# Convolution blocks of a two-layer kernel: normalised with channels or with tokens on the partitions

## The chip, the core and the metric

One core of a Trainium2 chip runs the whole program. The metric is the device time of one execution in microseconds (us). Tensor names are those of the kernel; P is 128, the number of partitions; S is 512, the number of tokens.

## The reference

Two transformer layers over 512 tokens of width 1024. The change touches the first layer's convolution branch: GLU, a causal depthwise convolution of 31 taps over 512 channels, LayerNorm over each group of 128 channels, then SiLU.

```python
def conformer_conv(val_b, gate_b, conv_w, conv_b, ln_g, ln_b):
    g = val_b * jax.nn.sigmoid(gate_b)
    c = lax.conv_general_dilated(g, conv_w[:, None, :], window_strides=(1,), padding=[(CONV_W - 1, 0)],
        dimension_numbers=('NWC', 'WIO', 'NWC'), feature_group_count=D_B)
    c = c + conv_b
    c = layer_norm(c.reshape(bsz, seq, H_B, HD_B), ln_g.reshape(H_B, HD_B), ln_b.reshape(H_B, HD_B))
    return jax.nn.silu(c).reshape(bsz, seq, D_B)

mix = jnp.concatenate([a_out, b_out], axis=-1)       # a_out: spatial gating of u and v
x = x + jnp.einsum('bsc,cd->bsd', mix, w_out[l])
```

The first layer goes on with a feed-forward block (FF1, FF2); the second layer has attention and another feed-forward block.

## The kernel before

Activations lie with channels on the partitions and the 512 tokens along the free dimension. Each fp32 product is taken as three fp32r matmuls: weights and activations are split into a high and a low part (high x high, high x low, low x high). The weights come as a stream of 512 KB chunks into four slots. SyncE loads them (`raw`), GpSimd splits them into `wh` and `wl` (L412, L415), TensorE uses them in the same order. GpSimd may split chunk n only when chunk n - 4 has been used (`chunk_done`). Its order, with extra jobs between chunks, is the table `after_chunk` (L506): multiplying GLU gates, ten taps of block 3 (`conv_taps`), and `head_low(0)`, `(1)`, `(2)`, which write the low part of the normed blocks 0 to 2 (semaphore `mixb_low`) after chunks `C_U+2`, `C_OUT1+3` and `C_OUT1+6`.

TensorE's order in the first layer is: eight GLU chunks, four V chunks with tokens on the partitions (`group_natural`, L571), four U chunks with the token mixing `mix_tokens` after each (L691), the product with `w_out` in three parts, then FF1. The three parts are `out1_first` (rows of the gating branch, eight tiles of 12 matmuls), `out1_heads` (convolution blocks 0 to 2, eight tiles of nine matmuls) and `out1_last` (block 3, eight tiles of three matmuls, four of them ahead of FF1 and four between its first matmuls).

VectorE's order is written out by hand from L1693. A convolution tap is one instruction over 128x512: the first two of a block are products (L1591, L1593), every further one adds to one of two accumulators in PSUM by turns (L1596). `conv(n)` issues the next n taps; the other jobs (`v_moments`, `u_scale`, `shifted_mix`, `gated`, `out1_first` and so on, the evictions and the gating) stand between them. VectorE does 114 taps and GpSimd ten.

The norm of a block runs as follows. `conv_center` (L680) subtracts the mean over channels by a fp32 matmul with a centering matrix, once for each accumulator (and once for GpSimd's part of block 3). `head_in` (L1187) squares and copies it on ScalarE, `norm_sums` (L625) takes the mean of squares with four matmuls of one column, `norm_sd` the root, `norm_factor` (VectorE) the reciprocal, `norm_spread` (L674) spreads it over the partitions by four transposes, `head_scale` (L1609) multiplies, and `head_out` (L1196) applies gain, bias and SiLU on ScalarE and copies the high part. `out1_heads` waits for `mixb_low` k + 1 ahead of its part k, and takes tiles 0 to 3 in two passes: blocks 0 and 1 of all four, then block 2 of all four (L807 to L812).

On ScalarE the functions Sqrt, Gelu and SiLU each need their own table (ACT_TABLE_LOAD); Copy and Identity need no change of it.

## Time and profile before

| | us |
|---|---|
| median of three runs | 1173.28 |
| lowest and highest | 1173.26, 1176.16 |
| the profiled execution | 1173.25 |
| its span, first to last instruction | 1171.5 |

The profile's page gives each engine's busy time (first part) and the trace a timeline, a table by stretches, and lists of who waited for whom. PE is TensorE's matmuls, PEld its weight loads, DVE VectorE, ACT ScalarE, POOL GpSimd. A matmul's duration overlaps the next one's: in a steady stream 128x512 fp32r matmuls of 0.39 us start 0.23 us apart. A fp32 matmul that isn't fp32r has two records in the trace for one instruction of the kernel (x2).

| stage of the first layer (TensorE) | from us | to us |
|---|---|---|
| GLU | 5.6 | 55.3 |
| V | 55.3 | 80.2 |
| U and mixing | 80.2 | 106.2 |
| out1, gating rows | 107.9 | 134.6 |
| out1, blocks 0 to 2 | 137.2 | 154.9 |
| out1, block 3, first four tiles | 154.9 | 157.6 |

### The profile page before, as it was taken

To read this page: it belongs to the slowest core of one execution; us is meant where nothing else is said; L and a number is where in the kernel's file an instruction comes from. 1 tells how busy PE (TensorE), PEld (TensorE's weight loads), DVE (VectorE), ACT (ScalarE), POOL (GpSimd) and SP (SyncE) were. 2 spreads that over 40 slices of the span, in tenths; PEclk is the share of its full clock that TensorE was granted. 3 is DMA by queue.
4 is the path that set the end of the run, shared out by engine and by line. 5 is a ranking of instruction groups with operands and counts; after the bars stand their busy time and mean duration, and the time that the engine had idled before them with its cause. 6 is when DMAs were issued, how large, how long until landed. Compare 5 with 4: busy or idle time off the path is not lost.

```text
span 1171.5 us, 15607 instructions
## 1 busy us (share of the span) xinstructions
PE 1152.4 (98%) x5394; PEld 929.9 (79%) x5394; DVE 609.0 (52%) x1005; ACT 291.0 (25%) x575; POOL 712.5 (61%) x436
## 2 busy tenths in 40 slices
PE   7999999999999999999999998999999999999997
PEld 5888788888888888888777776777888888888886
DVE  4999665530024443458789778847454001454114
ACT  5144352210001211120212346546421000221111
POOL 7879848666666666656455433226976666665660
PEclk9999999999999999999999999999999999999999
DMA  7321223322323223224433221112232322323312
GB/s 253 115 91 55 90 71 127 107 90 92 106 90 103 94 91 107 90 90 135 121 113 102 78 83 55 34 46 73 89 108 90 106 92 90 107 90 98 100 36 72
DMA packets 35760, 110.73 MB, mean 95 GB/s; under 512 B 4992, under 2 KB 7168, under 8 KB 35712
## 3 DMA queue, kind: packets, MB, share of 16 engines
q1 hardware_dynamic: 32352, 105.40, 27.0%
q10 hardware_dynamic: 3360, 4.69, 1.6%
q8 instruction: 30, 0.49, 0.2%
q14 instruction: 18, 0.15, 0.0%
HBM read 102.47 MB, written 2.10 MB: 89 GB/s over the span
## 4 chain that ended last, share of the span: by engine, by line
PE 92%; DVE 6%; issue 1%; ACT 1%; DMA 0%; DVEq 0%; SPq 0%; ACTq 0%
PE bank L554 25%; PE bank L556 25%; PE bank L555 25%; DVE bank L1596 2%; PE bank L926 2%; PE bank L586 1%; PE bank L585 1%; PE bank L587 1%; PE bank L619 1%; PE bank L611 1%; PE bank L612 1%; PE bank L940 1%; PE bank L968 1%; PE bank L884 1%; PE bank L964 1%
## 5 line engine op out<-in xcount | busy, mean ns | idle before, releaser
L415 POOL TENSOR_TENSOR wl<-raw,wh 128x1024 fp32r<-128x1024 f32 x188 | 454.8, 2419 | 15.7
L412 POOL TENSOR_SCALAR wh<-raw 128x1024 fp32r<-128x1024 f32 x188 | 202.8, 1079 | 394.8 <-PE bank L556 276.2
L554 PE MATMUL bank<-xh,wh 128*128 128x512 f32 x776 | 307.9, 397 | 0.4 <-ACT va L1332 0.4
L556 PE MATMUL bank<-xh,wl 128*128 128x512 f32 x776 | 302.5, 390 | 0.0
L555 PE MATMUL bank<-xl,wh 128*128 128x512 f32 x776 | 302.3, 390 | 0.0
L554 PE MATMUL bank<-uh,wh 128*128 128x512 f32 (+1 forms) x560 | 215.3, 384 | 0.0
L556 PE MATMUL bank<-uh,wl 128*128 128x512 f32 (+1 forms) x560 | 214.5, 383 | 0.0
L555 PE MATMUL bank<-ul,wh 128*128 128x512 f32 (+1 forms) x560 | 214.5, 383 | 0.0
L554 PEld LDWEIGHTS bank<-xh,wh 128*128 128x128 f32 x776 | 145.7, 188 | 45.7 <-issue 16.5
L1810 DVE TENSOR_TENSOR ul<-tmb,uh 128x512 f32 x64 | 124.7, 1948 | 90.1 <-ACT uh L1277 90.1
L556 PEld LDWEIGHTS bank<-xh,wl 128*128 128x128 f32 x776 | 145.7, 188 | 31.1
L555 PEld LDWEIGHTS bank<-xl,wh 128*128 128x128 f32 x776 | 145.8, 188 | 28.8 <-issue 0.2
L1276 ACT ACTIVATE tmb<-tmp 128x512 f32<-128x512 f32 x64 | 40.4, 632 | 413.3 <-DVE tmp L1807 413.3
L555 PEld LDWEIGHTS bank<-ul,wh 128*128 128x128 f32 x560 | 105.3, 188 | 20.8 <-issue 0.2
L556 PEld LDWEIGHTS bank<-uh,wl 128*128 128x128 f32 x560 | 105.2, 188 | 20.8
L554 PEld LDWEIGHTS bank<-uh,wh 128*128 128x128 f32 x560 | 105.3, 188 | 20.6 <-issue 0.2
L1807 DVE SCALAR_TENSOR_TENSOR tmp<-bank,rb 128x512 f32<-128x512 f32 x64 | 44.1, 688 | 70.7 <-PE bank L556 66.1
L1596 DVE SCALAR_TENSOR_TENSOR bank<-gpad,cols,bank 128x512 f32<-128x512 f32 x98 | 66.7, 749 | 0.0
L1821 DVE TENSOR_TENSOR x<-bank,x 128x512 f32 x8 | 5.5, 692 | 78.1 <-PE bank L556 78.1
L1823 DVE COPY y<-bank 128x512 f32 x8 | 5.5, 692 | 78.1 <-PE bank L556 78.1
L1277 ACT ACTIVATE uh<-tmp 128x512 f32 x64 | 39.5, 617 | 0.0
L585 PE MATMUL bank<-wh,xh 128*128 128x512 f32 x96 | 38.0, 395 | 0.0
(278 smaller groups left out, 1218.4 us busy)
## 6 DMA issues: line engine op xcount, KB each, us to landing
raw<-wstream SPq DMA_DIRECT2D x188, 512.0 KB, 3.3
x<-xT SPq DMA_DIRECT2D x8, 256.0 KB, 4.8
out<-x SPq DMA_DIRECT2D x16, 128.0 KB, 1.7
qi<-ropey ACTq DMA_DIRECT2D x16, 64.0 KB, 2.1
qd<-ropey ACTq DMA_DIRECT2D x16, 64.0 KB, 2.1
kd<-ropey ACTq DMA_DIRECT2D x16, 64.0 KB, 2.0
qa<-ropey SPq DMA_DIRECT2D x16, 64.0 KB, 2.0
ka<-ropey SPq DMA_DIRECT2D x16, 64.0 KB, 2.0
```

Of the source, the lines that this page charges most:

```text
L412: nc.gpsimd.tensor_scalar(wh[c][:], raw[c][:], 1.0, 1.0, ALU.mult, ALU.mult).then_inc(high_ready, 1)
L415: nc.gpsimd.tensor_tensor(wl[c][:], raw[c][:], wh[c][:].bitcast(F32), ALU.subtract).then_inc(split_ready, 1)
L554: mm(out, wh_, mh, start=start, stop=False)
L555: mm(out, wh_, ml, start=False, stop=False)
L556: return mm(out, wl_, mh, start=False, stop=stop)
L585: mm(out, xh[:, k, ts], wh[s][:, ws], start=k == 0, stop=False)
L926: mm(bank[4 + e][:, 0:N], q[r, h, tb * P:tb * P + P], k[r, h, 0:N], start=True, stop=True).then_inc(scores_done, 1)
L1276: A(tmb[c][:], tmp[c][:], ACT.Square).then_inc(square_ready, 1)
L1277: A(uh[:, bass.ds(r * 4 + c, 1), :].rearrange("p a n -> p (a n)"), tmp[c][:], ACT.Square).then_inc(uh_ready, 1)
L1596: ins = V.scalar_tensor_tensor(out=out, in0=src, scalar=w, in1=acc, op0=ALU.mult, op1=ALU.add)
L1807: V.scalar_tensor_tensor(out=tmp[c][:], in0=bank[c][:], scalar=0.0, in1=rb[:], op0=ALU.max, op1=ALU.mult).then_inc(evacuated, 1)
L1810: V.tensor_tensor(ul[:, bass.ds(r * 4 + c, 1), :].rearrange("p a n -> p (a n)"), tmb[c][:], uh[:, bass.ds(r * 4 + c, 1), :].rearrange("p a ...
```

## The change

The mean and the variance of a convolution block are taken with tokens on the partitions. VectorE adds the two accumulators (`conv_sum`), TensorE turns the block by four 128x128 transposes into `bank[4]` (`head_turn`), VectorE takes statistics over the 128 channels of each token (`head_moment`: four `bn_stats`, four `bn_aggr`), ScalarE the root (`head_root`), VectorE reciprocal and shift (`head_factors`), ScalarE norms in four instructions with scale and bias (`head_norm`), TensorE turns back into `NB` (`head_return`), and `head_out` reads that. Centering matrix, squares, one-column sums, spreads and `head_scale` go. The first two taps of blocks 1 to 3 are done by ScalarE (`head_first_taps`). The orders on TensorE, ScalarE and VectorE are written anew; blocks 0 to 2 of `out1_heads` are no longer taken in two passes. GpSimd's order stays; it builds two constants fewer. Semaphore counts shared with later norms are kept up by larger increments (`HEAD_NORMS`, left out below).

```diff
         vg = at("vg", [P, TB, 512], F32, uh_at + half + 8192)
-        conv_a = at("conv_a", [P, 2, S], F32, ul_at + half)
-        conv_o = at("conv_o", [P, 2, S], F32, ul_at + half + 4096)
+        conv_s = at("conv_s", [P, 2, S], F32, ul_at + half)
...
+            def head_turn(h):
+                pe.wait_ge(conv_summed, h + 1)
                 if h:
-                    pe.wait_ge(cm_ready, h)
-                pe.wait_ge(conv_step, (h + 1) * TAPS - (POOL_TAPS if h == 3 else 0))
-                mm(bank[4][:], center[:], conv_a[:, h % 2], start=True, stop=False)
-                if h == 3:
-                    pe.wait_ge(conv_pool, POOL_TAPS)
-                    mm(bank[4][:], center[:], conv_p[:], start=False, stop=False)
-                mm(bank[4][:], center[:], conv_o[:, h % 2], start=False, stop=True).then_inc(centered, 1)
+                    pe.wait_ge(head_normed, TB * h)
+                for t in range(TB):
+                    ts = slice(t * P, t * P + P)
+                    last = nc.tensor.transpose(bank[4][:, ts], conv_s[:, h % 2, ts], ident[:])
+                last.then_inc(head_turned, 1)
+            def head_return(h):
+                pe.wait_ge(head_normed, TB * (h + 1))
+                if h == 0:
+                    pe.wait_ge(mix_shifts, 4)
+                else:
+                    pe.wait_ge(silu_ready, h)
+                for t in range(TB):
+                    ts = slice(t * P, t * P + P)
+                    last = nc.tensor.transpose(NB[:, ts], cm[:, h % 2, ts], ident[:])
+                last.then_inc(head_returned, 1)
...
-            group_natural(C_V, 0, E_V - 4, between=(lambda: conv_center(0), first_head_sums, lambda: norm_spread(1)))
...
-                chunk_transposed(n % SLOTS, bank[m][:], xh, xl)
+                chunk_transposed(n % SLOTS, bank[m][:], xh, xl, hooks={4: lambda: head_turn(1)} if m == 0 else {})
                 if m:
                     mix_tokens(m - 1)
             mix_tokens(3)
-            conv_center(1)
+            head_return(1)
...
-                    if 3 * o + k in (5, 15, 23):
+                    if 3 * o + k in (7, 15, 23):
...
             for o in range(8):
                 out1_first(o)
-                if o == 0:
-                    norm_sums(2, sq[1], 1, head_sq, 2)
-                if o == 1:
-                    norm_spread(2)
-                if o == 3:
-                    conv_center(2)
                 if o == 4:
-                    norm_sums(3, sq[0], 1, head_sq, 3)
-                if o == 5:
-                    norm_spread(3)
-            conv_center(3)
+                    head_turn(2)
+                if o == 6:
+                    head_return(2)
             for o in range(4):
-                out1_heads(o, range(2))
-            norm_sums(4, sq[1], 1, head_sq, 4)
-            for o in range(4):
-                out1_heads(o, range(2, 3))
-            norm_spread(4)
-            for o in range(4, 8):
+                out1_heads(o, range(3))
+            head_turn(3)
+            for o in range(4, 6):
+                out1_heads(o, range(3))
+            head_return(3)
+            for o in range(6, 8):
                 out1_heads(o, range(3))
             for o in range(4):
                 out1_last(o)
...
-            def head_in(h):
-                act.wait_ge(centered, h + 1)
+            def head_first_taps(j):
+                act.wait_ge(conv_summed, j)
+                act.wait_ge(glu_ready, j + 1)
+                t = POOL_TAPS if j == 3 else 0
+                A(conv_acc[0][:], gpad[:, j, t:t + S], ACT.Identity, scale=col("conv_w", j * TAPS + t),
+                  bias=col("conv_b", j)).then_inc(first_taps, 1)
+                t += 1
+                A(conv_acc[1][:], gpad[:, j, t:t + S], ACT.Copy, scale=col("conv_w", j * TAPS + t)
+                  ).then_inc(first_taps, 1)
+            def head_root(h):
+                act.wait_ge(head_moments, TB * (h + 1))
+                A(head_mv[:, :, 2:3], head_mv[:, :, 1:2], ACT.Sqrt, bias=eps[:, 0:1]).then_inc(head_std, 1)
+            def head_norm(h):
+                act.wait_ge(head_factor, h + 1)
                 if h >= 2:
-                    act.wait_ge(bc_used, h)
-                    act.wait_ge(sums_done, h)
-                A(sq[h % 2][:], bank[4][:], ACT.Square).then_inc(head_sq, 1)
-                A(cm[:, h % 2], bank[4][:], ACT.Copy).then_inc(cm_ready, 1)
+                    act.wait_ge(head_returned, h - 1)
+                for t in range(TB):
+                    ts = slice(t * P, t * P + P)
+                    A(cm[:, h % 2, ts], bank[4][:, ts], ACT.Identity, scale=head_mv[:, t, 3:4],
+                      bias=head_mv[:, t, 4:5]).then_inc(head_normed, 1)
             def head_out(h):
-                act.wait_ge(bc_used, h + 2)
+                act.wait_ge(head_returned, h + 1)
                 if h >= 2:
                     act.wait_ge(mixb_low, h - 1)
                 else:
                     act.wait_ge(glu_ready, h + 3)
                 out = bank[4] if h == 3 else tmb[2 + h % 2]
-                A(out[:], tmp[2 + h % 2][:], ACT.Silu, scale=col("conv_g", h), bias=col("conv_lb", h)
+                A(out[:], NB[:], ACT.Silu, scale=col("conv_g", h), bias=col("conv_lb", h)
                   ).then_inc(silu_ready, 1)
...
             for j in range(4):
                 sigmoid(j)
-            head_in(0)
-            norm_sd(1)
+            head_first_taps(1)
+            head_root(0)
+            head_norm(0)
             head_out(0)
             for t in range(TB):
                 v_gelu(t)
+            head_first_taps(2)
             act.wait_ge(v_stats, TB)
             A(mvs[:, :, 2:3], mvs[:, :, 1:2], ACT.Sqrt, bias=eps[:, 0:1]).then_inc(v_std, 1)
+            head_root(1)
             act.wait_ge(v_factor, 1)
             for t in range(TB):
                 A(vg[:, t], vg[:, t], ACT.Identity, scale=mvs[:, t, 3:4], bias=mvs[:, t, 4:5]).then_inc(v_normed, 1)
+            head_norm(1)
             for h in range(4):
                 u_gelu(h)
                 if h:
                     a_high(h - 1)
             a_high(3)
-            head_in(1)
-            norm_sd(2)
             head_out(1)
             A(soft[:, 0:1], eps[:, 0:1], ACT.Sqrt).then_inc(table_loaded, 1)
-            head_in(2)
-            norm_sd(3)
+            head_first_taps(3)
+            head_root(2)
+            head_norm(2)
             head_out(2)
             A(soft[:, 0:1], eps[:, 0:1], ACT.Sqrt).then_inc(table_loaded, 1)
-            head_in(3)
-            norm_sd(4)
+            head_root(3)
+            head_norm(3)
             head_out(3)
...
             steps = [0]
-            DVE_TAPS = [(j, t) for j in range(4) for t in range(POOL_TAPS if j == 3 else 0, TAPS)]
...
-                        dve.wait_ge(centered, j - 1)
-                    acc = conv_acc[i % 2][:]
+                    acc = conv_acc[first % 2][:]
                     src = gpad[:, j, t:t + S]
                     w = col("conv_w", j * TAPS + t)
-                    if i >= 2:
+                    if j and first < 4:
+                        dve.wait_ge(first_taps, 2 * (j - 1) + first - 1)
+                    elif i >= 2:
                         dve.wait_ge(conv_step, i - 1)
                     if first == 0:
                         ins = V.tensor_scalar(acc, src, w, col("conv_b", j), ALU.mult, ALU.add)
                     elif first == 1:
                         ins = V.tensor_scalar(acc, src, w, None, ALU.mult)
                     else:
-                        out = (conv_o if t % 2 else conv_a)[:, j % 2] if t >= TAPS - 2 else acc
+                        if t == TAPS - 2 and j >= 2:
+                            dve.wait_ge(head_turned, j - 1)
+                        out = conv_s[:, j % 2] if t == TAPS - 2 else acc
                         ins = V.scalar_tensor_tensor(out=out, in0=src, scalar=w, in1=acc, op0=ALU.mult, op1=ALU.add)
                     ins.then_inc(conv_step, 1)
                 steps[0] += taps
+            def conv_sum(j):
+                assert steps[0] == len([1 for jj, _ in DVE_TAPS if jj <= j])
+                dve.wait_ge(conv_step, steps[0])
+                total = conv_s[:, j % 2]
+                if j < 3:
+                    V.tensor_tensor(total, conv_acc[0][:], total, ALU.add).then_inc(conv_summed, 1)
+                else:
+                    link(V.tensor_tensor(conv_acc[0][:], conv_acc[0][:], total, ALU.add))
+                    dve.wait_ge(conv_pool, POOL_TAPS)
+                    V.tensor_tensor(total, conv_acc[0][:], conv_p[:], ALU.add).then_inc(conv_summed, 1)
+            def head_moment(h):
+                dve.wait_ge(head_turned, h + 1)
+                for t in range(TB):
+                    V.bn_stats(head_stats[:, t, 0:6], bank[4][:, t * P:t * P + P]).then_inc(head_counted, 1)
+                for t in range(TB):
+                    dve.wait_ge(head_counted, TB * h + t + 1)
+                    V.bn_aggr(head_mv[:, t, 0:2], head_stats[:, t, 0:6]).then_inc(head_moments, 1)
+            def head_factors(h):
+                dve.wait_ge(head_std, h + 1)
+                dve.wait_ge(head_moments, TB * (h + 1))
+                link(V.reciprocal(head_mv[:, :, 3:4], head_mv[:, :, 2:3]))
+                V.scalar_tensor_tensor(out=head_mv[:, :, 4:5], in0=head_mv[:, :, 0:1], scalar=-1.0,
+                                       in1=head_mv[:, :, 3:4], op0=ALU.mult, op1=ALU.mult).then_inc(head_factor, 1)
             def u_scale(j):
                 dve.wait_ge(chunk_done, C_U + j + 1)
...
                     dve.wait_ge(sig_ready, 4)
                 mul(tmp[j % 2][:], bank[j % 4][:], rb[:]).then_inc(evacuated, 1)
-            def head_scale(h):
-                dve.wait_ge(bc_done, h + 2)
-                if h >= 2:
-                    dve.wait_ge(silu_ready, h - 1)
-                mul(tmp[2 + h % 2][:], cm[:, h % 2], NB[:]).then_inc(bc_used, 1)
             def head_low(h):
                 dve.wait_ge(mixb_high, h + 1)
...
             gate(3)
             conv(1)
+            conv_sum(0)
             shift_of_mix()
-            conv(18)
-            norm_factor(1)
-            conv(8)
-            head_scale(0)
-            conv(8)
+            conv(10)
+            head_moment(0)
+            conv(4)
+            head_factors(0)
+            conv(15)
+            conv_sum(1)
             for t in range(TB):
                 v_moments(t)
-            conv(3)
+            head_moment(1)
+            u_scale(0)
+            conv(2)
             v_factors()
-            u_scale(0)
-            conv(7)
+            head_factors(1)
+            conv(4)
             u_scale(1)
             conv(1)
             shifted_mix(0)
...
             gated_low(0)
             conv(4)
             u_scale(2)
-            conv(1)
             shifted_mix(1)
             gated(1)
             conv(1)
             gated_low(1)
-            conv(3)
+            conv(4)
             u_scale(3)
             shifted_mix(2)
             gated(2)
...
             gated(3)
             conv(1)
             gated_low(3)
-            conv(4)
+            conv(2)
             out1_first(0)
-            conv(2)
-            norm_factor(2)
-            conv(2)
+            conv(3)
             out1_first(1)
-            head_scale(1)
             conv(3)
             out1_first(2)
             conv(3)
+            conv_sum(2)
             out1_first(3)
-            conv(6)
+            conv(3)
             out1_first(4)
+            conv(3)
+            head_moment(2)
+            out1_first(5)
             conv(2)
-            norm_factor(3)
+            head_factors(2)
             conv(2)
-            out1_first(5)
-            head_scale(2)
+            out1_first(6)
             conv(3)
-            out1_first(6)
             out1_first(7)
-            assert steps[0] == 4 * TAPS - POOL_TAPS
-            norm_factor(4)
-            for k in range(4):
+            conv(3)
+            out1_heads(0)
+            conv(3)
+            conv_sum(3)
+            for k in range(1, 4):
                 out1_heads(k)
-            head_scale(3)
+            head_moment(3)
             out1_heads(4)
+            head_factors(3)
             out1_heads(5)
             head_low(3)
```

## Rows read from the trace of the kernel before

**Rows 1.** Page, first part: busy time, share of the span, instructions of each engine
```profile
PE 1152.4 (98%) x5394; PEld 929.9 (79%) x5394; DVE 609.0 (52%) x1005; ACT 291.0 (25%) x575; POOL 712.5 (61%) x436
```

**Rows 2.** Table by stretch: us, then busy us of each engine, granted clock, DMA share, GB/s
```profile
55.00:80.00 25.00, 25.00 (x114) 20.08 (x114) 24.86 (x42) 8.77 (x12) 16.36 (x10) 1.00 0.26 89
80.00:105.00 25.00, 24.84 (x122) 20.84 (x120) 24.70 (x44) 9.95 (x14) 23.68 (x16) 1.00 0.22 79
105.00:137.00 32.00, 31.78 (x143) 24.10 (x143) 28.82 (x47) 14.14 (x20) 30.97 (x21) 1.00 0.18 59
```

**Rows 3.** Who waited for whom, TensorE, whole run: us in total, times, longest
```profile
PE bank L611 <- ACT xh L1168: 5.6, 1, 5.6
PE bank L940 <- DVE probs L2023: 1.9, 3, 1.2
...
PE bank L697 <- DVE tmp L1502: 0.3, 1, 0.3
```

**Rows 4.** Who waited for whom, GpSimd, 80.54 to 139.45 us: the only entry
```profile
POOL wh L412 <- PE bank L587: 1.1, 1, 1.1
```

**Rows 5.** Timeline, GpSimd: start us, us, engine line op out<-in, idle before
```profile
80.54 1.05 POOL L412 TENSOR_SCALAR wh<-raw 128x1024 fp32r<-128x1024 f32 x1 [1.10 <-PE bank L587]
...
138.15 1.30 POOL L475 TENSOR_TENSOR ul<-tmb,uh 128x512 fp32r<-128x512 f32 x1
```

**Rows 6.** Timeline, TensorE: centering, sums, spread, and the start of FF1
```profile
60.71 1.02 PE L685 MATMUL bank<-conv_a,center 128*128 128x512 f32 x2
...
62.66 0.40 PE L586 MATMUL bank<-wl,xh 128*128 128x512 f32 x1
...
67.92 0.95 PE L631 MATMUL bank<-inv,sq 128*128 128x1 f32 x8
...
69.05 0.39 PE L586 MATMUL bank<-wl,xh 128*128 128x512 f32 x1
...
74.30 0.60 PE L671 MATMUL bank<-ident,rn 128*128 128x128 f32 x4
...
74.97 0.39 PE L586 MATMUL bank<-wl,xh 128*128 128x512 f32 x1
...
157.62 0.39 PE L611 MATMUL bank<-xh,wh 128*128 128x512 f32 x1
```

**Rows 7.** One line of the kernel: attention's turns, ns min/median/max, first and last start
```profile
L940 PE MATMUL bank<-ident,probs x120: 270/272/330, 649.5 to 777.1; 128*128 128x128 f32 x120
```

**Rows 8.** Timeline, VectorE
```profile
56.73 1.12 DVE L1640 SCALAR_TENSOR_TENSOR mix_shift<-bank,cols,rows 128x128 f32<-128x128 f32 x4
...
69.76 5.33 DVE L1596 SCALAR_TENSOR_TENSOR bank<-gpad,cols,bank 128x512 f32<-128x512 f32 x8
...
78.89 0.81 DVE L1591 TENSOR_SCALAR bank<-gpad,cols 128x512 f32<-128x512 f32 x1
...
80.92 0.69 DVE L1625 BATCH_NORM_STATS2 stats<-vg 128x6 f32<-128x512 f32 x1
81.64 0.18 DVE L1626 BATCH_NORM_AGGREGATE mvs<-stats 128x2 f32<-128x6 f32 x1
...
93.85 0.70 DVE L1502 TENSOR_TENSOR bank<-bank,ug 128x512 f32<-128x512 f32 x1
...
104.45 0.68 DVE L1502 TENSOR_TENSOR tmp<-bank,rb 128x512 f32<-128x512 f32 x1
```

**Rows 9.** Timeline, ScalarE
```profile
86.70 2.94 ACT L1237 ACTIVATE vg<-vg,mvs 128x512 f32<-128x512 f32 x4 [2.15 <-DVE mvs L1632]
89.65 1.28 ACT L1211 ACT_TABLE_LOAD   x1
```

**Rows 10.** Timeline, TensorE, shortly after its first matmul
```profile
9.25 0.63 PE L612 MATMUL bank<-xh,wl 128*128 128x512 f32 x1
...
10.04 0.39 PE L611 MATMUL bank<-xh,wh 128*128 128x512 f32 x1
10.27 0.40 PE L612 MATMUL bank<-xh,wl 128*128 128x512 f32 x1
```

More of the change, by code:

```diff
@@ L43 @@
 POOL_TAPS = 10
+HEAD_NORMS = 4
 HEADS = 8
@@ L636, in norm_sums @@
                                   start=True, stop=True)
-                last.then_inc(sums_done, 1)
+                last.then_inc(sums_done, 1 + HEAD_NORMS if i == 0 else 1)
             def head_sums(h):
@@ L1150, in norm_rb @@
                 act.wait_ge(bc_done, i + 1)
-                A(out[:], NB[:], ACT.Copy).then_inc(bc_used, 1)
+                A(out[:], NB[:], ACT.Copy).then_inc(bc_used, 1 + HEAD_NORMS if i == 0 else 1)
             squares = [0]
@@ L1573, in _ @@
             steps = [0]
-            DVE_TAPS = [(j, t) for j in range(4) for t in range(POOL_TAPS if j == 3 else 0, TAPS)]
+            DVE_TAPS = [(j, t) for j in range(4) for t in range((POOL_TAPS if j == 3 else 0) + (2 if j else 0), TAPS)]
             def conv(taps):
```

45 lines of the change are left out of this document (20 added, 25 removed).

## The prediction

> **What bounds the kernel now.** The page's first part comes first: TensorE is busy for 98% of the span, so a change pays only where it takes work or waiting off TensorE [rows 1]. The table by stage then shows the part that the change touches, 55 to 157 us. From 55 to 137 us two engines are nearly full at once: TensorE without gaps, and VectorE for 24.86 of 25, 24.70 of 25 and 28.82 of 32 us; GpSimd joins them from 80 us (23.68 of 25, 30.97 of 32) [rows 2]. The list of waits has only one entry of TensorE between 24 and 157 us, the 0.3 us ahead of the last mixing matmuls [rows 3]. GpSimd waited once between 80.54 and 139.45 us, at its start, for the last V matmul, and then ran without a wait up to the low part of convolution block 2 [rows 4, 5]. That start and that end carry the forecast. Everything after about 158 us (FF1 onward) the change leaves alone, and TensorE bounds it, so I let a shift at the start of FF1 pass 1:1 to the end.
>
> **TensorE: what goes and what comes.** A centering is two fp32 128x512 matmuls: the first starts at 60.71 us, and the first V matmul in regular step behind it at 62.66 (0.23 a matmul) instead of 60.94, so 1.72 us; block 3 has a third, 2.58. Four make 7.7 us. The four sums with one column: 67.92 to 69.05 less 0.23 is 0.90 us, four 3.6. The four spreads: 74.30 to 74.97 less 0.23 is 0.44, one with a small wait, 2.0 in all [rows 6]. Removed: 13.4 us. Added are eight groups of four 128x128 transposes. The nearest rows are the spreads (same form, 0.44 a group) and the 120 turns of attention's probabilities, which carry data as these do, 272 ns long and pipelined [rows 6, 7]. I take 0.44, together 3.5 us; the ends are 0.44 and four times 0.272, 1.09. The net is 9.9 us: 1173.25 - 9.9 = 1163.4 if TensorE alone decided.
>
> The rows show 272 ns as a duration that overlaps its neighbours. The Trainium skill (TensorE: Matmul & The Clock Gate, Part 4: PE-mode transpose) puts a 128x128 bf16 transpose at about 275 ns inside a kernel; the duration agrees, but if this were also the distance from one to the next, the groups would cost 8.8 us, an estimate, and the net 4.6.
>
> **VectorE.** Gone: six first taps, about 0.69 each (0.72 and 0.66), 4.1 us; four scalings of 512 elements, 0.60 each in step (0.70 long, as the products are), 2.4; four reciprocals, 0.4. Added: five sums of the two accumulators at 0.60 to 0.69, 3.1; sixteen statistics over 128 elements, sixteen aggregations at 0.10 in step, and four pairs of factors, 0.35 each. The statistics' price isn't in the trace: 512 elements take 0.66, another 128-element instruction takes 0.26 in step. Bounds 0.10 and 0.66; I take 0.22, as the length scales [rows 8]. A block's moments are then 4 x 0.22 + 4 x 0.10 + 0.1 for the first wait = 1.4 us. Added: 3.1 + 5.6 + 1.4 = 10.1, net 3.2 us more on an engine that had no slack from 57 to 134 us. Six taps move behind `out1_first(6)`, where it did have slack.
>
> **ScalarE.** Four normalising instructions replace Square and Copy. Four of 512 elements with scale and bias take 2.94 us; less 384 elements at 0.83 ns each leaves 0.4, so 1.6 us a block. A tap 0.75. The table for Gelu or Silu loads only behind them, 1.28 [rows 9].
>
> **Along the stages.** (1) Up to V. V0 ends at 60.71. `conv_sum(0)` is done at 57.5, so the turn costs 0.44. VectorE: mix shifts to 58.5, ten taps at 0.655 to 65.1, moments 66.5, four taps 69.1, factors 69.5; ScalarE's norm is ready at 71.2. TensorE reaches `head_return(0)` at 61.15 + 2 x 5.44 = 72.03, no wait, 0.8 us of margin. V3 ends at 77.9 where it ended at 80.2: 2.3 us early (1.72 - 0.44 and 0.90, remainder rounding; spread against return is even).
>
> (2) GpSimd. Its unbroken run starts with V3's end, 2.3 us early, and none of its conditions (chunks 13 to 18 done, `mixb_high`) comes later than its own pace. `head_low(2)`, 138.15 to 139.45 now, then ends at 137.2 [rows 5]. No edit touches this order.
>
> (3) Gelu and mixing. VectorE after the factors of block 0: fifteen taps and `conv_sum(1)` to 80.0, V moments 83.2, head moments 84.6, `u_scale(0)` 85.2, two taps, `v_factors` 87.15, factors 87.5. ScalarE's V norm ends at 90.1 and `head_norm(1)` at 91.7 now stands ahead of the Gelu table: first Gelu done at 93.6 (before, the table loaded at 89.65 and the first Gelu was done at 91.6), so `gated(0)` starts at 93.65 against 93.85 and VectorE waits 1.5 us. `mix_tokens(0)` waits until 90.1, 0.85 us on TensorE. `u_scale(3)` ends at 104.9 against 105.05, so the last mixing starts only about 0.2 us early [rows 8, 9]. TensorE's lead has gone into waits for VectorE and ScalarE.
>
> (4) First half of out1. Its first tile ends at 110.1, as against 110.67. Without the sums and the spread, `out1_first(6)` ends at 126.9. VectorE: two taps, then a tile and three taps in turn, `conv_sum(2)` 119.4, moments 126.3, factors 128.6; ScalarE's norm 130.2. `head_return(2)` stands in TensorE's queue ahead of `out1_first(7)`, so TensorE waits about 3.4 us. Return 130.7, `out1_first(7)` 133.4, two parts of `out1_heads(0)` 134.8.
>
> (5) The gate. The third part needs `mixb_low` 3, because blocks 0 to 2 are no longer taken in two passes. Silu and copy are ready at 133, but GpSimd delivers at 137.2. TensorE waits 2.4 us. From there: 0.68, three tiles of 2.04 to 144.0, turn 144.4, two tiles 148.5; VectorE: tile 3, moments 146.1, tile 4, factors 147.65; norm 149.3, so `head_return(3)` waits 0.8; 149.8, two tiles: 153.9. Before, this point lay at 154.9 (four `out1_last` tiles of 0.68 ahead of FF1's 157.62) [rows 6]. Block 3's Silu, copy and low part end at 152.7, ahead of their reader.
>
> Shift: 1.0 us. Span 1170.5, time 1173.25 - 1.0 = 1172.2. The profiled execution is 1.75 us longer than its span and equals the median (1173.28) for this purpose.
>
> **Rivals.**
>
> A, *the last norm is hidden*: as above, but `head_return(3)` finds it ready. 149.0 + 4.08 = 153.1, 1.8 us early: 1171.4. This is also the floor that the GpSimd gate allows.
>
> B, *small instructions cost more than their length*: statistics at the upper bound, 0.66. Each block's moments grow by 1.6 us. `head_return(0)` then waits 0.8, V3's end and the gate go to 138.0; up to block 2 VectorE is 4.8 us later, more than the 2.4 us of slack at the gate, so TensorE passes it at 139.7; block 3 adds another 1.6. Sum: -1.0 + 2.5 + 1.6 = +3.1, time 1176.3, slower. For it: nothing shows 128-element statistics. Against: other 128-element rows scale down [rows 8]. It turns the sign once moments cost about 0.9 us more than I take. Transposes 0.27 apart would add 0.65 at each of two groups ahead of V's end and of two behind the gate: 1174.8.
>
> C, *TensorE's clock falls in the new waits*. At the start, after 5.6 us of idling, matmuls take 0.63 us and come about 0.4 us apart until 10 us, then 0.39 long and 0.23 apart, which fits 1.2 and then 2.4 GHz (the granted-clock column itself reads 1.00 over this stretch, so I go by the matmuls). The nine slow ones cost about 1.8 us [rows 3, 10]. The new waits are 3.4 and 2.4 us, the longest since then. A slow stretch after the first is absorbed by the gate; one after the second costs 1.8: 1174.0, slower than now. Within the kernel's body no wait was longer than 1.2 us [rows 3], so nothing here shows what 3 us do.
>
> The Trainium skill (TensorE: Matmul & The Clock Gate, Part 1) says that an idle spell throttles the array back to half rate until it has been busy again, which speaks against a change that trades matmuls for waits; no row here shows it inside the kernel.
>
> D, *TensorE alone decides*: 9.9 us less, 1163.4. It would need `mixb_low` 3 at 127 us, while GpSimd is full to 137.
>
> **How the numbers follow.** Forecast 1172.2: 45%. A 15%. B 15%, of which I give half a result beyond 1176.8. C 18%. D and anything else below 1169.8: 7%. The predicted time is 1172.2. The range takes in A's floor with 0.6 below it and reaches B's price: 1170.6 to 1176.3. About 0.3%, 3.5 us, is what a measurement tells from no change. Faster by more: 7%. Slower by more (above 1176.8): half of B and a case of B with C, 11%. Within: 82%.
>
> **What would show it.** TensorE's waits in 80 to 150 us: one under 1 us before the first mixing, one of about 3 us before the transposes of `head_return(2)`, one of 2 to 3 us before a matmul of `out1_heads(0)`, released by GpSimd's low part at 137.2, one under 1 us before `head_return(3)`. Transposes in step of 0.11. Statistics in step of 0.22. V3's last matmul about 2.3 us earlier. FF1's first matmul at 156.6. Wrong would be: GpSimd's run broken by a wait, statistics above 0.4, or matmuls 0.4 us apart after the waits.

## The result, and the profile after the change

| us | before | changed |
|---|---|---|
| median, 19 executions of each | 1173.37 | 1175.56 |
| lowest and highest | 1173.14, 1176.16 | 1175.35, 1176.56 |
| the profiled execution, its span | 1173.25, 1171.5 | 1176.56, 1174.8 |
| FF1's first matmul starts | 157.62 | 160.91 |

The ratio is 1.0018, 95% interval 1.0012 to 1.0024: 2.2 us slower, where 1.1 us faster was forecast. The profiled span grew by 3.3 us, and FF1 starts 3.3 us later, so all of it arises before FF1, as [rows 6] let it be read. The profiled execution of the changed kernel is its longest, 1.0 us above its median, so times read from this trace overstate the median's loss by about that much.

TensorE's work did fall. First the page's first part, then the list of waits of TensorE from 20 to 162 us, its only entries (us in total, times, longest):

```profile
PE 1147.6 (98%) x5360; PEld 927.1 (79%) x5360; DVE 614.5 (52%) x1036; ACT 295.5 (25%) x588; POOL 711.5 (61%) x434
```

```profile
PE bank L700 <- ACT cm L1210: 3.7, 2, 3.1
PE bank L709 <- ACT vg L1257: 3.4, 1, 3.4
PE bank L761 <- ACT uh L1241: 1.2, 1, 1.2
```

Busy time fell by 4.8 us against [rows 1], and that although some matmuls ran slower (below); [rows 3] had one wait of 0.3 in this stretch, now there are 8.3 us. L709 is the mixing, which waits for ScalarE's norm of V, L700 the return of a block, L761 the first half of out1. The table by stretch (granted clock third from the right) names the second loss:

```profile
90.00:105.00 15.00, 11.91 (x49) 10.15 (x50) 12.49 (x21) 8.25 (x14) 14.38 (x11) 0.77 0.21 70
105.00:120.00 15.00, 13.77 (x70) 11.23 (x70) 14.74 (x23) 6.34 (x9) 14.57 (x11) 1.00 0.13 47
120.00:135.00 15.00, 12.15 (x56) 9.72 (x54) 14.68 (x31) 3.00 (x7) 14.48 (x10) 1.00 0.25 81
135.00:140.00 5.00, 4.75 (x16) 3.85 (x17) 2.56 (x4) 4.38 (x6) 2.37 (x2) 0.66 0.42 147
```

Behind each of the two long waits the clock falls. The timeline of TensorE:

```profile
93.09 2.08 PE L709 MATMUL bank<-sguw,vg 128*128 128x128 f32 x8 [3.37 <-ACT vg L1257]
...
95.39 0.63 PE L556 MATMUL bank<-xl,wh 128*128 128x512 f32 x1
95.82 0.63 PE L557 MATMUL bank<-xh,wl 128*128 128x512 f32 x1
...
135.25 0.66 PE L700 MATMUL bank<-ident,cm 128*128 128x128 f32 x4 [3.11 <-ACT cm L1210]
...
136.75 0.63 PE L762 MATMUL bank<-uh,wl 128*128 128x512 f32 x1
137.18 0.63 PE L761 MATMUL bank<-uh,wh 128*128 128x512 f32 x1
```

Matmuls 0.63 long and 0.43 apart (1.2 GHz) in place of 0.39 and 0.23 (2.4 GHz), until 98.4 and again until about 139.3.

What made V's norm late stands on VectorE. Its timeline, then GpSimd's, of the same microseconds:

```profile
87.32 0.18 DVE L1674 RECIPROCAL mvs<-mvs 128x4 f32<-128x4 f32 x1
87.53 0.17 DVE L1522 TENSOR_TENSOR mvs<-mvs 128x4 f32<-128x4 f32 x1
87.74 2.34 DVE L1676 TENSOR_SCALAR mvs<-mvs 128x4 f32<-128x4 f32 x1
89.99 0.17 DVE L1647 RECIPROCAL head_mv<-head_mv 128x4 f32<-128x4 f32 x1
90.19 0.54 DVE L1648 SCALAR_TENSOR_TENSOR head_mv<-head_mv 128x4 f32<-128x4 f32 x1
```

```profile
87.66 2.39 POOL L416 TENSOR_TENSOR wl<-raw,wh 128x1024 fp32r<-128x1024 f32 x1
90.03 1.56 POOL L490 TENSOR_SCALAR ss<-gpad,cols 128x512 f32<-128x512 f32 x1
```

Each of these instructions handles four numbers per partition, and the last of the three instructions takes 2.34 us. It started 0.08 us behind a GpSimd split and ended (90.08) with it (90.05). V's norm therefore ends at 93.0, not 90.1.

### The profile page after: what moved, and what is told of

Same layout as the page of the kernel before. It is cut to its first block, busy times and chain, and to the rows that moved or that the text cites. A ratio compares the mean times of both kernels' runs of the same rounds, so it can differ in the third digit from the quotient of the medians.

```text
span 1174.8 us, 15580 instructions
## 1 busy us (share of the span) xinstructions
PE 1147.6 (98%) x5360; PEld 927.1 (79%) x5360; DVE 614.5 (52%) x1036; ACT 295.5 (25%) x588; POOL 711.5 (61%) x434
## 4 chain that ended last, share of the span: by engine, by line
PE 90%; DVE 7%; ACT 1%; issue 1%; DMA 0%; DVEq 0%; SPq 0%; ACTq 0%
PE bank L555 26%; PE bank L556 25%; PE bank L557 25%; DVE bank L1618 3%; PE bank L926 2%; PE bank L587 1%; PE bank L586 1%; PE bank L588 1%; PE bank L620 1%; PE bank L612 1%; PE bank L613 1%; PE bank L940 1%; PE bank L968 1%; PE bank L884 1%; PE bank L964 1%
## 5 line engine op out<-in xcount | busy, mean ns | idle before, releaser
L1618 DVE SCALAR_TENSOR_TENSOR bank<-gpad,cols,bank 128x512 f32<-128x512 f32 x102 | 69.9, 748 | 0.3 <-ACT bank L1192 0.3
L1875 DVE TENSOR_TENSOR y<-bank,y 128x512 f32<-128x512 f32 x7 | 4.8, 692 | 62.7 <-PE bank L557 62.7
```

The lines of the kernel that those rows point to most:

```text
L1618: ins = V.scalar_tensor_tensor(out=out, in0=src, scalar=w, in1=acc, op0=ALU.mult, op1=ALU.add)
```

## The experiments

Two theories stood at the start. The port (for the access to SBUF that the two engines would share): a small VectorE instruction with both operands, or source and target, in SBUF stands still while a GpSimd split runs, and its price isn't 0.17 but what is left of GpSimd's. The clock: the waits would be harmless, and what costs is the half rate behind them. Two rivals: the turns, statistics and norms themselves cost more than taken; or the order of the work around the return of block 2 is to blame.

**port_free.** The second operand of each pair of factors comes from PSUM, which holds a second copy of the reciprocal. V's factors are formed in the same way: two reciprocals and one product with -1 in place of reciprocal, product and negation. VectorE also waits (`silu_ready`) until `NB` is free to hold the copy.

```diff
-link(V.reciprocal(head_mv[:, :, 3:4], head_mv[:, :, 2:3]))
+if h:
+    dve.wait_ge(silu_ready, h)
+V.reciprocal(head_mv[:, :, 3:4], head_mv[:, :, 2:3])
+link(V.reciprocal(NB[:, 0:4].unsqueeze(2), head_mv[:, :, 2:3]))
 V.scalar_tensor_tensor(out=head_mv[:, :, 4:5], in0=head_mv[:, :, 0:1], scalar=-1.0,
-                       in1=head_mv[:, :, 3:4], op0=ALU.mult, op1=ALU.mult).then_inc(head_factor, 1)
+                       in1=NB[:, 0:4].unsqueeze(2), op0=ALU.mult, op1=ALU.mult).then_inc(head_factor, 1)
...
```

> The changed kernel, with the factors of the V norm and of the convolution norms formed so that no VectorE instruction on 128x4 has two SBUF inputs or goes from SBUF to SBUF with a constant: the reciprocal is also written to PSUM and the product reads it there. Theory 1 (the small instructions wait for a GpSimd instruction in flight: 2.34 us for a negation of 128x4, ended 0.03 us behind GpSimd's): each takes 0.2 us, the V norm starts near 87.4 instead of 90.1 us, the wait before the first mixing falls from 3.4 to about 0.9 us, the granted clock stays full from 90 to 105 us, and the time is 1172.3 to 1173.3 us (the second wait of about 3 us stays). Theory 2 (the small instructions are slow for a reason of their own, or VectorE has no time for them anyway): durations of 0.5 to 2.3 us stay or the lead is lost elsewhere, 1175.5.

Measured: 1172.77 us (1172.56 to 1174.37), ratio to before 0.9994, interval 0.9985 to 1.0004; span 1170.8, where the forecast had 1170.5. Its waits of TensorE from 20 to 162 us:

```profile
PE bank L700 <- ACT cm L1210: 3.1, 2, 2.5
PE bank L555 <- POOL ul L476: 1.7, 1, 1.7
PE bank L761 <- ACT uh L1241: 1.0, 1, 1.0
PE bank L709 <- DVE tmp L1522: 0.8, 1, 0.8
PE bank L612 <- issue: 0.2, 1, 0.2
```

The wait of 3.4 for V's norm is gone, and the gate of the forecast is there. GpSimd's timeline and TensorE's at that point:

```profile
135.99 1.26 POOL L476 TENSOR_TENSOR ul<-tmb,uh 128x512 fp32r<-128x512 f32 x1
```

```profile
137.40 0.47 PE L555 MATMUL bank<-uh,wh 128*128 128x512 f32 x1 [1.73 <-POOL ul L476]
```

The clock still fell behind the wait of 2.5 (0.89 in the stretch from 120 to 135 us), but the gate swallowed it. FF1 starts at 157.01. So 3.9 of the 4.3 us between the forecast's 156.6 and the changed kernel's 160.91 go with four VectorE instructions of 128x4; by the medians it is 2.8 us (1175.56 to 1172.77). V's factors need care here. They ran from 86.20 to 86.64, before the split began at 87.61, because block 0's pair no longer lost 1.35 us. Whether freeing block 0's pair alone would do the same wasn't tried. Nor is port_free faster than before, clear of noise: its interval includes no change.

**port_v.** The same for V's factors alone.

> The changed kernel with the second operand of V's factors alone taken from PSUM (the head blocks' pairs of factors stay as the change has them). If the loss comes from the one instruction that stood 2.34 us behind GpSimd's split, V's factors are done near 86.5, the mixing doesn't wait for ScalarE's norm, and the time is that of the kernel with both kinds of factors from PSUM but for the part of block 2, whose pair was stretched by 0.7: head_return(2) waits 3.1 to 3.3 (2.5 there) and the gate of 137.4 swallows that again, so 1172.8 to 1173.3. If the head blocks' pairs are a cause of their own, half of the 2.8 us or more stays: 1174.2 or above.

Measured: 1173.13 us (1172.73 to 1174.48), ratio 0.9997, 0.9987 to 1.0006; the wait of L700 3.3. The first range, 1172.8 to 1173.3, holds in time but not in every step: V's factors were done at 87.85, not 86.5, since block 0's pair still took its 1.51, and the mixing waited 1.1 us for V's norm, where no wait was expected. Its timeline shows the theory better than its time does. VectorE, with block 0 and then V and block 1:

```profile
69.23 1.51 DVE L1648 SCALAR_TENSOR_TENSOR head_mv<-head_mv 128x4 f32<-128x4 f32 x1
...
87.69 0.16 DVE L1677 SCALAR_TENSOR_TENSOR mvs<-mvs,bank 128x4 f32<-128x4 f32 x1
87.77 0.18 DVE L1647 RECIPROCAL head_mv<-head_mv 128x4 f32<-128x4 f32 x1
87.98 2.18 DVE L1648 SCALAR_TENSOR_TENSOR head_mv<-head_mv 128x4 f32<-128x4 f32 x1
```

and GpSimd:

```profile
68.33 2.39 POOL L416 TENSOR_TENSOR wl<-raw,wh 128x1024 fp32r<-128x1024 f32 x1
...
87.74 2.40 POOL L416 TENSOR_TENSOR wl<-raw,wh 128x1024 fp32r<-128x1024 f32 x1
```

The head factors, left in SBUF, took over the stretch of 2.18 and again ended with the split (90.16 and 90.14). In port_free the same instruction with a PSUM operand ran at the same moment, inside the same split, in 0.16 (VectorE, then GpSimd):

```profile
69.22 0.16 DVE L1651 SCALAR_TENSOR_TENSOR head_mv<-head_mv,bank 128x4 f32<-128x4 f32 x1
```

```profile
68.25 2.41 POOL L416 TENSOR_TENSOR wl<-raw,wh 128x1024 fp32r<-128x1024 f32 x1
```

1.51 against 0.16 is the cleanest pair: same data, same start, same neighbour. V's own factors, at 87.69, are no such proof, since they started just before the split. The other traces repeat both halves. Block 2's product with both operands in SBUF took 0.86 (changed kernel), 1.03 (port_v), 1.66 (warm) and 0.60 us (two_pass), and each time its end lay within 0.03 us of the end of a GpSimd instruction. In the changed kernel that was the first half of a split, which makes `wh` (VectorE, then GpSimd):

```profile
132.80 0.86 DVE L1648 SCALAR_TENSOR_TENSOR head_mv<-head_mv 128x4 f32<-128x4 f32 x1
```

```profile
132.60 1.04 POOL L413 TENSOR_SCALAR wh<-raw 128x1024 fp32r<-128x1024 f32 x1
```

With the operand in PSUM it took 0.16 inside a split in nine_same too (127.55). The theory is too wide at one point: the reciprocal goes from SBUF to SBUF, and in the changed kernel it took 0.17 at 68.93, inside a split that began at 68.23.

**warm.** The changed kernel, with three fp32 matmuls on constants in front of the first mixing and three in front of `head_return(2)`, so that TensorE works instead of waiting.

```diff
+                if m == 1:
+                    pe.wait_ge(evacuated, E_U + 1)
+                    keep_warm(3)
                 if m:
                     mix_tokens(m - 1)
...
                 if o == 6:
+                    pe.wait_ge(evacuated, E_OUT1 + 4)
+                    keep_warm(3, 3)
                     head_return(2)
```

> The changed kernel, with three fp32 matmuls of no use (0.86 us each) put ahead of the first mixing and three ahead of the turning back of block 2, where TensorE waited 3.4 and 3.1 us. Theory 1 (half of the loss is the clock): the granted clock stays at its full level in 90 to 105 and 135 to 140 us, the 12 and 9 matmuls that were 0.43 us apart come 0.23 apart, and the time is 1172.5 to 1173.2. Theory 2 (what counts is only when VectorE and ScalarE deliver): the time stays at 1175.5, the waits only move behind.

Measured: 1174.01 us (1173.90 to 1174.64), ratio 1.0001, 0.9991 to 1.0011. VectorE's instruction is as slow as before (2.34 at 88.02), the same norm is awaited, but no clock falls. The table by stretch and the mixing in TensorE's timeline:

```profile
90.00:105.00 15.00, 14.24 (x66) 10.78 (x65) 13.73 (x23) 8.58 (x14) 14.38 (x11) 1.00 0.21 70
...
135.00:140.00 5.00, 5.00 (x24) 4.10 (x24) 3.84 (x7) 3.59 (x5) 4.01 (x4) 1.00 0.43 153
```

```profile
93.38 1.16 PE L709 MATMUL bank<-sguw,vg 128*128 128x128 f32 x8 [0.76 <-ACT vg L1262]
```

FF1 starts at 158.50, 2.4 us before that of the changed kernel, and the profiled span is 2.5 shorter (1172.3). The median gained 1.6. So the two falls of the clock cost 1.6 us together by the medians and up to 2.4 in the profiled execution, and matmuls that compute nothing gave it back. I had expected 1172.5 to 1173.2, so the clock was worth less than I thought.

**port_warm.** Both edits.

> Both edits: the factors by way of PSUM, and the matmuls of no use ahead of the first mixing and of the turning back of block 2. If the port and the clock together are the whole difference from the forecast, the time is 1172.2 (1171.8 to 1172.6), the forecast for the change. If a third cause is at work, it stays at 1173 or above. The three matmuls ahead of the first mixing may be longer than the wait that is left there and cost up to 1.5 us of TensorE, which the wait at block 2 should absorb.

Measured: 1172.86 us (1172.62 to 1174.12), ratio 0.9992, 0.9983 to 1.0002, FF1 at 157.02, the gate's wait 1.7 again. That lies between my two cases (1171.8 to 1172.6, or 1173 and above). Against port_free nothing is gained: the one fall left there (behind the wait of 2.5) lies in front of the gate. Here the gate sets the time and the clock doesn't.

**two_pass.** The changed kernel, with `head_return(2)` behind `out1_first(7)`, the first four tiles of the heads in two passes (blocks 0 and 1, then block 2), `head_turn(3)` between them, and `head_return(3)` behind the fifth tile. VectorE's order follows.

```diff
...
-                if o == 6:
+                if o == 7:
                     head_return(2)
             for o in range(4):
-                out1_heads(o, range(3))
+                out1_heads(o, range(2))
             head_turn(3)
-            for o in range(4, 6):
-                out1_heads(o, range(3))
+            for o in range(4):
+                out1_heads(o, range(2, 3))
+            out1_heads(4, range(3))
             head_return(3)
...
```

> The changed kernel with TensorE's order in out1 altered: block 2 is turned back behind out1_first(7) instead of ahead of it, tiles 0 to 3 of the convolution rows are taken in two passes again (blocks 0 and 1, then block 2), block 3 is turned between the passes and turned back behind tile 4; VectorE's order follows. The waits at the factors and the first clock loss stay. If the order around block 2 is where the change loses its 10 us of TensorE work, the second wait shrinks from 3.1 to under 1 us, the second clock loss goes, and the time is 1170.2 (1169.5 to 1171.5). If VectorE is the bound whatever the order, it is 1174 to 1175.5.

Measured: 1173.97 us (1172.84 to 1175.46), ratio 0.9998, 0.9989 to 1.0008. The wait for block 2 is gone, and a wait of 2.2 for block 3's sum has taken its place; behind it the clock falls too (TensorE's timeline):

```profile
143.56 1.12 PE L688 MATMUL bank<-ident,conv_s 128*128 128x128 f32 x4 [2.24 <-DVE conv_s L1633]
144.33 0.78 PE L555 MATMUL bank<-uh,wh 128*128 128x512 f32 x1
144.91 0.63 PE L556 MATMUL bank<-ul,wh 128*128 128x512 f32 x1
```

So the order was worth something (1.6 by the medians), but far from the 1170.2 that I had expected: my first order of it turned block 3 too early. The four small instructions were left as slow as they were.

**nine_taps, nine_same.** With port_free's factors: one tap of block 3 moved from GpSimd to VectorE, to test the gate. nine_taps leaves out more than the expectation for nine_same says. With nine taps on GpSimd the two accumulators change places, and the sum still reads the first one: it counts ten taps twice and leaves out eleven. nine_same reads the other one and has all 31. Both issue the same instructions over the same sizes.

```diff
-POOL_TAPS = 10
+POOL_TAPS = 9
...
             out1_heads(0)
-            conv(3)
+            conv(4)
             conv_sum(3)
```

and in nine_same also

```diff
-                    link(V.tensor_tensor(conv_acc[0][:], conv_acc[0][:], total, ALU.add))
+                    link(V.tensor_tensor(conv_acc[0][:], conv_acc[1][:], total, ALU.add))
```

> With both kinds of factors from PSUM, and one tap of block 3 moved from GpSimd to VectorE. It tests the gate of the forecast: that GpSimd's unbroken run ends with head_low(2) at 137.2 and that TensorE's first use of that part waits for it. GpSimd has about 2.1 us less to do (a product of 1.57 and a sum), VectorE 0.66 more. If the gate holds as a price, TensorE's wait for GpSimd's low part (1.7 us at 137.40) goes to 0, what remains late is the return of block 2 (a wait of 2.5 in front of it), and the time falls by 1.0 to 1.7: 1171.1 to 1171.8. If the gate hides a wait that appears elsewhere (the turn or return of block 3, or VectorE's added tap), it stays within 0.4 of 1172.8.

> The kernel with both kinds of factors from PSUM and nine taps of block 3 on GpSimd, its sums now taken so that all 31 taps are in. The run with nine taps showed FF1's first matmul at 155.8 (157.0 with ten taps) but a median 2.9 us lower, 1.7 more than that step. If the 1.7 belong to the moved tap, the time is 1169.7 again. If they came from the part of the block that was missing there (the last tap of block 3 was outside the sum), or from an execution to execution difference behind FF1, FF1 starts at 155.8 again and the time is 1171.3 to 1171.8. The same for the gate itself in both cases: TensorE has no wait for GpSimd's low part of block 2.

Measured: nine_taps 1169.85 us (1169.66 to 1173.15), ratio 0.9967, 0.9955 to 0.9980; nine_same 1170.67 (1169.50 to 1172.77), ratio 0.9975, 0.9965 to 0.9984. In nine_same GpSimd starts the low part at 132.92 where port_free had 135.99, TensorE has no wait for it any more, and FF1 starts at 155.03, 2.0 earlier; the median is 2.1 lower. The gate was real, and its price slightly above the wait that showed it. Both expectations missed in time: nine_taps came out below its 1171.1, and nine_same between its two cases (1169.7, or 1171.3 to 1171.8). I had argued from nine_taps' profiled execution, and that was an odd one, 1173.15 where the other five took 1169.7 to 1170.8. In it VectorE lost 2.1 us early on (last section), and FF1 started at 155.80, 0.8 later than in nine_same. Behind FF1 it lost another 1.8 us, in the second layer's attention, where the granted clock was 0.50 from 725 to 730 us (nine_same 1.00). Why nine_taps' median is 0.8 below nine_same's stays open. The sum that it leaves out saves no instruction, and both kernels have executions at 1169.5 to 1169.8.

**two_late, two_again.** port_free's factors, the two passes, but `head_turn(3)` behind the second pass and `head_return(3)` behind the sixth tile. It ran twice. TensorE's order against that of two_pass:

```diff
             for o in range(4):
                 out1_heads(o, range(2))
-            head_turn(3)
             for o in range(4):
                 out1_heads(o, range(2, 3))
+            head_turn(3)
             out1_heads(4, range(3))
+            out1_heads(5, range(3))
             head_return(3)
```

> With both kinds of factors from PSUM, block 2 returned behind the last first-half tile, the heads' products of the first four tiles in two passes (parts 0 and 1, then part 2), block 3 turned after the second pass and returned before the seventh tile. It removes both what TensorE waits for ahead of the heads: 2.5 us before the return of block 2 and 1.7 at GpSimd's gate. If these waits are on the path and nothing stands behind them, FF1 starts 4.2 us earlier than at 157 and the time is 1168.6 to 1169.5. If the chain of block 3 is next (its sum is done near 143.5, and turn, statistics, root, norm, return, SiLU, copy and low part take some 7.5 us before its product can start), or GpSimd's splits of the next weights, only 1 to 2.5 us are gained: 1170.3 to 1171.8.

> The kernel with two passes and block 3 turned late once more, on the chip of the kernels with nine taps: FF1's first matmul at 152.1, 5.5 us before that of the kernel before, so 1167.8 to 1169.6 and a ratio of 0.995 to 0.996. A ratio above 0.9975 would say that the first result was one of its few runs.

Measured: 1168.63 (1167.73 to 1169.61), ratio 0.9958, 0.9941 to 0.9974, and 1168.69 (1167.94 to 1169.34), ratio 0.9957, 0.9940 to 0.9973. No chain of block 3 stood behind. One kernel, and its eight executions lie at 1167.7 to 1168.1 or 1169.3 to 1169.6. The two profiled ones, one of each kind, show what differs in them (TensorE's timeline at the gate, two_late, then two_again):

```profile
137.48 0.47 PE L555 MATMUL bank<-uh,wh 128*128 128x512 f32 x1 [1.06 <-POOL ul L476]
137.79 0.40 PE L556 MATMUL bank<-ul,wh 128*128 128x512 f32 x1
```

```profile
137.46 0.63 PE L555 MATMUL bank<-uh,wh 128*128 128x512 f32 x1 [2.00 <-POOL ul L476]
137.88 0.63 PE L556 MATMUL bank<-ul,wh 128*128 128x512 f32 x1
```

The gate opens at the same moment. TensorE reached it 0.9 us earlier in the second, waited 2.0 instead of 1.1, lost its clock, and started FF1 at 153.70 instead of 152.13. Arriving early cost 1.6 us. That the other six divide in the same way is likely, but no trace shows it.

**two_norm.** two_late, and ScalarE norms block 1 behind its last copy of the gated half, to reach the first GELU sooner. TensorE turns block 1 back behind the second tile of the gating rows (left out below).

```diff
-            head_norm(1)
             for h in range(4):
                 u_gelu(h)
                 if h:
                     a_high(h - 1)
             a_high(3)
+            head_norm(1)
             head_out(1)
...
```

> As the kernel with two passes and block 3 turned late, and in addition ScalarE norms block 1 behind its last copy of the gated half, and TensorE returns it behind the second first-half tile. ScalarE reaches the first GELU 1.5 us earlier (VectorE waited 1.3 for it before gated(0)). If the gated half is on the path into the first output tiles, TensorE's wait for its low part (1.0 us) goes and the time is 0.6 to 1.3 below that kernel. If VectorE's own order (the scalings of U and the taps) sets the first output tile, it is within 0.4 of it, and if block 1's later low part reaches the heads, above it.

Measured: 1169.36 (1167.76 to 1169.70), ratio 0.9962, 0.9948 to 0.9976. The lowest execution and both profiled spans (1166.0) are those of two_late, the medians of so few executions 0.7 apart. By the profiled executions that is the second case; by the medians the third isn't excluded. TensorE's waits in the gating rows are 1.5 us there (1.0 in two_late), so ScalarE's place in front of the first GELU gained nothing.

**two_nine.** two_late with nine taps on GpSimd, summed as in nine_same.

> The kernel with two passes and block 3 turned late (FF1 at 152.1, TensorE waits 1.1 us for GpSimd's low part of block 2, between the first and the second pass), with nine taps on GpSimd. If that wait is the last that stands in front of the heads, FF1 starts at 151.0 and the time is 1.1 us below the kernel with ten taps. If VectorE's tap, 0.66 more before the sum of block 3, moves the turn of block 3 and through it the last product, the gain is 0.4 or less.

Measured: 1166.02 us, all four executions between 1165.94 and 1166.15, ratio 0.9936, 0.9919 to 0.9953. It beats both kernels, by 7.6 us against the 1173.62 of before in these runs. TensorE's waits from 20 to 162 us:

```profile
PE bank L761 <- ACT uh L1243: 1.0, 1, 1.0
PE bank L709 <- DVE tmp L1524: 0.8, 1, 0.8
PE bank L612 <- issue: 0.2, 1, 0.2
```

FF1 starts at 150.43, 7.2 us before that of the kernel before. I expected 151.0 and a gain of 1.1 us; the median gained 2.7 over two_again. Part of it is the upper of two_again's two levels, which is missing here: TensorE doesn't wait at the gate any more, and in the profiled execution its clock stays full from 20 to 150 us. Against the lower level of the kernel with ten taps the gain is 1.7 to 2.1 us.

## Why the prediction was wrong, point by point

**The step that failed: "four pairs of factors, 0.35 each", and V's three at their old price.** Block 0's pair took 0.17 and 1.52, V's last 2.34, block 1's second 0.54, block 2's 0.86; only block 3's stayed at 0.17, and it had started 0.03 us ahead of GpSimd's next instruction (151.82 and 151.85). The first delay led to the longest one. Block 0's 1.35 us too many let V's factors begin at 87.32 (86.20 in port_free), GpSimd's run came 2.0 us earlier than in before, and the two met in a split. With these instructions at 0.15 to 0.18 us each (port_free), the sum was right to 0.3 us in the span and 0.6 in the median. I scaled small instructions by their length and took [rows 8] as the nearest. The nearest by what they read was a row of before that I left out, an SBUF to SBUF instruction of 128x4 (VectorE, then GpSimd, kernel before):

```profile
25.34 1.67 DVE L1539 COPY rn<-rn 128x4 f32<-128x4 f32 x1
```

```profile
24.59 2.40 POOL L415 TENSOR_TENSOR wl<-raw,wh 128x1024 fp32r<-128x1024 f32 x1
```

It ends at 27.01, the split at 26.99. The page of before had it in its fifth part too: the same subtraction over 128x512, once with two SBUF operands in the feed-forward blocks, and in the split of x with one in PSUM (the second line is from the groups by line):

```profile
L1810 DVE TENSOR_TENSOR ul<-tmb,uh 128x512 f32 x64 | 124.7, 1948 | 90.1 <-ACT uh L1277 90.1
```

```profile
L1546 DVE TENSOR_TENSOR xl<-bank,xh 128x512 fp32r<-128x512 f32 x8 | 5.5, 692 | 9.9 <-ACT bank L1171 9.9
```

1948 against 692 ns, and the one that ran inside a split (12.31, the split 11.15 to 13.53) took 0.69 like the rest. The Trainium skill (SBUF — State Buffer, Who interferes with whom) says that a VectorE instruction with two SBUF inputs, or a copy or tensor_scalar in its two-port mode, contends with GpSimd, and that whoever comes first holds the shared ports for the whole instruction; port_free and port_v agree, 0.16 against 1.51. It doesn't show everywhere: in before V's three factors took 0.17 each beside a GpSimd tap, at 86.07 to 86.66. What a tap does isn't settled: block 1's factors took 0.54 beside one, at 90.19.

**Rival C, the clock in the new waits (18%).** Right in mechanism, wrong in place. It had the clock fall behind `head_return(2)`, absorbed by the gate, and behind the gate, 1.8 us. In the changed kernel it fell behind the mixing's wait (3.4, where 0.85 was forecast) and behind `head_return(2)` (3.1, 3.4 forecast), and there nothing absorbed it: GpSimd itself waited 1.95 us for SiLU's copy, its low part came at 139.3 in place of 137.2, and TensorE found it ready. The two falls cost 1.6 us by the medians and up to 2.4 in the profiled execution (warm). The absorbed fall is what port_free shows, and there the clock stayed full behind the gate's wait of 1.7.

**Rival B, dearer small instructions (15%).** Its time, 1176.3, is nearest to the measured one, by the wrong instructions. Statistics took 0.89 for four, as 0.22 each had it; aggregations 0.36. Turns: four in 0.60, the next matmul 0.35 to 0.42 behind, against 0.44 taken. ScalarE's norm of a block took about 1.5 (1.6 forecast). That the sign came out as B had it is luck.

**Stages.** (1) nearly held: `head_return(0)` waited 0.03, so the margin of 0.8 was eaten by block 0's 1.52, and V3's end lay 2.0 us early (2.3 forecast). (2) GpSimd's run began 2.0 early (78.54 against 80.54 in [rows 5]), but the 1.95 for SiLU's copy broke it in front of `head_low(2)`; in port_free it had no such wait and `head_low(2)` ended at 137.25, as forecast. (3) failed: factors done 90.08, not 87.15; first matmul of the mixing 93.1; last scaling of U begun at 108.65, not 104.3. (4) `head_return(2)` at 135.25, not 130.2. (5) no gate wait, as TensorE was later than the gate; `head_return(3)` waited 0.57 (0.8). In port_free each of these came within about 0.9 us of the forecast: gate 1.7 (2.4), return of block 2 129.29, FF1 157.01 (156.6).

**Rival D (7%)** needed the low part at 127 us. Freed at both waits and at the gate, TensorE gained 7.2 of the 9.9 us (two_nine), with 1.8 us of waits left: most of the ceiling was real, and GpSimd's one tap, the order of the heads and the small instructions stood between.

## What to carry to other kernels

A small instruction on a path that others wait for costs what its operands allow: before pricing it by its length, look whether GpSimd runs beside it and whether VectorE reads two operands in SBUF (or goes from SBUF to SBUF with a constant or a copy), and take one of them from PSUM. Look also at where a delay moves the instructions behind it: here it moved V's factors into a split. Freed time turns into waits, and waits of 2.0 us and more cost the clock here; fill them with other work, or with matmuls that compute nothing. Look for the gate behind the saving (here GpSimd's low part, which one tap held back) before counting the saving.

## What the runs showed of the hardware

The same instruction in the same kernel took 2.90 or 0.69 us by 0.1 us of arrival. The product of the first GLU block, VectorE and GpSimd in two_late:

```profile
31.59 2.90 DVE L1524 TENSOR_TENSOR gpad<-gpad,tmb 128x512 f32<-128x512 f32 x1
```

```profile
31.55 2.39 POOL L416 TENSOR_TENSOR wl<-raw,wh 128x1024 fp32r<-128x1024 f32 x1
```

and in two_again:

```profile
31.55 0.69 DVE L1524 TENSOR_TENSOR gpad<-gpad,tmb 128x512 f32<-128x512 f32 x1
```

```profile
31.61 2.91 POOL L416 TENSOR_TENSOR wl<-raw,wh 128x1024 fp32r<-128x1024 f32 x1
```

Whoever is first goes at its own pace, the other ends about 0.5 to 2.2 us late. All thirteen traces have this pair and agree: VectorE started first in ten and took 0.69, GpSimd in three (nine_taps, two_late, two_norm) and took 2.39. After it VectorE did block 0's factors at 70.02 in two_late and at 68.89 in two_again, and only in two_late did TensorE wait 0.9 us for V's norm: the race fits TensorE's later arrival at the gate. That it makes the levels of the other kernels' executions too wasn't shown.

Of TensorE's waits from 20 to 162 us, those of 2.0, 2.2, 2.5, 3.1, 3.3 and 3.4 us were followed by 1.2 GHz, those of 1.7, 1.3 and below were not. The Trainium skill (TensorE: Matmul & The Clock Gate, Part 1) has idling bring the half rate; these rows agree, and the shortest wait that did so is 2.0. A long wait isn't the only way to lose the clock: in nine_taps it fell to 1.2 GHz from 725 to 730 us, among attention's small matmuls, and from 715 us on no wait was longer than 0.4 us.
